# Grouping four dense tiles of the delta rule's preparation into two visits of two

## The reference

```python
def chunk_gated_delta_rule(q, k, v, g, beta):
    ...
    decay = jnp.exp(jnp.where(causal, g[..., :, None] - g[..., None, :], -jnp.inf))
    lower = jnp.where(strict, jnp.einsum('bhncd,bhnmd->bhncm', k_beta, k) * decay, 0.0)
    a_mat = lower + jnp.eye(C, dtype=jnp.float32)
    rhs = jnp.concatenate([v_beta, k_beta * jnp.exp(g)[..., None]], axis=-1)
    sol = lax.linalg.triangular_solve(a_mat, rhs, left_side=True, lower=True, unit_diagonal=True)
    ...
    qk = jnp.einsum('bhncd,bhnmd->bhncm', q, k) * decay
    ...
# in the same layer, independent of the delta rule:
gate_b, gate_c, hv = sc_in[..., :SC_WIDTH], sc_in[..., SC_WIDTH:2 * SC_WIDTH], sc_in[..., 2 * SC_WIDTH:]
y = gate_b * causal_depthwise_conv(gate_c * hv, sc_conv_w)
```

## Time and profile before

| | us |
|---|---|
| median of 3 runs | 3553.3 (3548.85, 3553.3, 3554.7) |
| the profiled execution, its own time | 3546.45 |
| its span, first to last instruction | 3544.6 |
| preparation of the first layer, on PE | 2293.3 to 2328.0 |
| preparation of the second layer, on PE | 2972.2 to 3006.9 |

### The profile page before, as it was taken

One profiled execution on the slowest core, in us unless ns is written; L12 is line 12 of the kernel. 1 busy time (PEld: TensorE's weight loads), 2 busy tenths in 40 slices (PEclk: granted clock), 3 DMA queues, 4 the chain that ended last, 5 costly groups with the idle time before them and its releaser, 6 DMA issues. The chain is left out here.

```text
span 3544.6 us, 44743 instructions
## 1 busy us (share of the span) xinstructions
PE 3472.5 (98%) x18492; PEld 2827.2 (80%) x18492; DVE 1985.0 (56%) x2961; ACT 1203.7 (34%) x1890; POOL 149.8 (4%) x212
## 2 busy tenths in 40 slices
PE   9999999999999999999999999999999999999999
PEld 6878877688888888877688887788888888788887
DVE  5565576775466755666763366675423366652233
ACT  3222334632233222334632234633322254342222
POOL 1110100001000110100000001000000000000000
PEclk9999999999999999999999999999999999999999
DMA  8663341245343653331333242212233322123332
GB/s 287 220 196 115 96 106 48 90 152 188 124 153 114 215 177 115 98 104 49 90 121 124 87 154 57 72 37 78 84 96 119 101 61 66 43 73 100 95 98 87
DMA packets 438048, 397.84 MB, mean 112 GB/s; under 512 B 53780, under 2 KB 390276, under 8 KB 437845
## 3 DMA queue, kind: packets, MB, share of 16 engines
q1 hardware_dynamic: 413028, 310.53, 29.0%
q0 software_dynamic: 24816, 84.45, 7.0%
HBM read 390.14 MB, written 4.78 MB: 111 GB/s over the span
## 5 line engine op out<-in xcount | busy, mean ns | idle before, releaser
L175 PE MATMUL m_ps<-m_h_high,ffn_w_high 128*128 128x512 f32 x2064 | 806.8, 391 | 4.9 <-DVE ffn_w_low L182 4.9
L177 PE MATMUL m_ps<-m_h_high,ffn_w_low 128*128 128x512 f32 x2064 | 803.6, 389 | 0.0
L176 PE MATMUL m_ps<-m_h_low,ffn_w_high 128*128 128x512 f32 x2064 | 803.3, 389 | 0.0
L175 PEld LDWEIGHTS m_ps<-m_h_high,ffn_w_high 128*128 128x128 f32 x2064 | 387.4, 188 | 87.4 <-issue 7.1
L177 PEld LDWEIGHTS m_ps<-m_h_high,ffn_w_low 128*128 128x128 f32 x2064 | 387.4, 188 | 81.2
L176 PEld LDWEIGHTS m_ps<-m_h_low,ffn_w_high 128*128 128x128 f32 x2064 | 387.6, 188 | 79.2
L1062 ACT ACTIVATE ffn_sil<-m_ps 128x512 f32<-128x512 f32 x132 | 79.0, 599 | 1087.4 <-PE m_ps L177 1087.4
L175 PE MATMUL m_ps<-ffn_w_high,ffn_hid_high 128*128 128x512 f32 x1056 | 411.6, 390 | 0.0
L177 PE MATMUL m_ps<-ffn_w_high,ffn_hid_low 128*128 128x512 f32 x1056 | 411.0, 389 | 0.0
L176 PE MATMUL m_ps<-ffn_w_low,ffn_hid_high 128*128 128x512 f32 x1056 | 410.9, 389 | 0.0
L182 DVE TENSOR_TENSOR ffn_w_low<-m_raw,ffn_w_high 128x2048 fp32r<-128x2048 f32 (+1 forms) x138 | 296.3, 2150 | 120.2 <-ACT ffn_w_high L1056 117.4
(11 more groups left out here) (511 smaller groups left out, 5375.4 us busy)
## 6 DMA issues: line engine op xcount, KB each, us to landing
m_raw<-in_ffn_w SPq DMA_DIRECT2D x176, 512.0 KB, 4.8
ffn_rows<-in_ada_w POOLq DMA_DIRECT2D x128, 512.0 KB, 5.0
ffn_rows<-in_ffn_w SPq DMA_DIRECT2D x88, 512.0 KB, 3.5
m_raw<-in_w_in SPq DMA_DIRECT2D x32, 1024.0 KB, 5.2
m_raw<-in_ffn_w_gate SPq DMA_DIRECT2D x44, 512.0 KB, 3.7
m_raw<-in_ffn_w_up SPq DMA_DIRECT2D x44, 512.0 KB, 4.8
ffn_rows<-in_ffn_w_down SPq DMA_DIRECT2D x44, 512.0 KB, 3.3
m_raw<-in_w_out SPq DMA_DIRECT2D x24, 512.0 KB, 4.4
```

Source lines behind the costliest of these rows:

```text
L175: pe.matmul(out, sh, mh, start=first, stop=False, skip_group_check=True)
L176: pe.matmul(out, sh, ml, start=False, stop=False, skip_group_check=True)
L177: return pe.matmul(out, sl, mh, start=False, stop=last, skip_group_check=True)
```

## The change

On PE the call of `dense` behind every token tile goes; behind token tiles 1 and 3 (the second and the fourth) two dense tiles are now computed, 0 and 1, then 2 and 3. On ACT `evacuate` stands in turns 1 and 3, for both tiles. On DVE it stands in turn 2 for tiles 0 and 1, and behind the loop for tiles 2 and 3. No instruction is added or taken away, and no buffer changes.

```diff
@@ PE, end of the turn of token tile i
                 mm.then_inc(S.v_turned, 1)
-                dense(i)
+                if i % 2:
+                    dense(i - 1, i)
@@ ACT, turn i
                 act.activation(A.D[:, i], A.D[:, i], ACT.Exp).then_inc(S.decay, 1)
-                evacuate(i)
+                if i % 2:
+                    evacuate(i - 1)
+                    evacuate(i)
                 act.wait_ge(S.q_scaled, i + 1)
@@ DVE, turn i, between diff and the lower triangle
-                if i:
+                if i and i % 2 == 0:
+                    evacuate(i - 2)
                     evacuate(i - 1)
                 dve.wait_ge(S.decay, i + 1)
@@ DVE, behind the four turns
+            evacuate(TT - 2)
             evacuate(TT - 1)
```

## The result

Over nine runs of each, the changed kernel takes 3563.3 us in the median and the kernel before 3550.9: +12.4 us, ratio 1.0031 with a 95% interval of 1.0022 to 1.0039. It is slower, by 0.2 to 0.4%. The forecast was 12.4 us more than before.

A forecast was written before the change was run, and what follows sets the result against it. PE, busy 98% of the span, was taken as the bound. Per layer 6.57 us of waits - 0.54 for the mask + 0.19 small terms gave 6.2, for two 12.4: 3565.7 us against median 3553.3, range 3558 to 3573.

The forecast's parts named there:

- PE sets the end, DVE's chain is covered by the dense tiles: Four turns: only PE's idle time counts; dense tiles (5.55 us) hide DVE's 6.5 us chain, token tiles take PE 3.45.
- Token tile 1, 2.68 us: Second token tile, uncovered: PE waits for DVE's differences, lt_ready, nat_ready and prep_free, 2.68 us a layer in all.
- the 10.4 that I named: Expected profile row: PE's waits at L2748 on DVE's second triangle product, 5.2 us a layer (1.7 and 3.6).
- Token tile 3, 3.89 us, and the 2.86 us of DVE work in it: Fourth token tile: PE waits 3.89 us a layer; low part, copy and low part put 2.86 us before tile 2's triangle.
- The short waits for `nat_ready` and `prep_free`: Before each dense pair, PE waits 0.18 us for one DVE product and 0.15 us for the next.
- The mask, -0.54: Start of the levels: PE's old wait on DVE's first mask (L2784) goes, -0.54 us a layer.
- Small terms, +0.19: Slower first instructions behind seven new waits, less a missing changeover in each dense pair: together +0.19 us a layer.
- the 0.35 us for restarts: First instruction behind a wait takes 0.65 instead of 0.60 us; seven new waits give +0.35 us.
- The sum: Both layers together: 6.2 us a layer, 12.4 us in all, giving 3565.7 us against the earlier median.
- Rival A: Levels and behind: PE's existing waits take up the delay, leaving 3.1 us in all, 3556.4 us; chance 0.10.
- the counter-argument: Against regained waits: L175's 1.5 us and the recurrence's waits depend on PE's own earlier work, so they move with it.
- Rival B: Token tile 3: PE's clock halves behind the 3.56 us wait, +3.0 us a layer, 18.4 in all, 3571.7 us; chance 0.06.

The follow-up runs named there:

- e2_evac_only: Kernel before, with only the ACT and DVE evacuations moved as in the change, dense tiles left behind every token tile; 3558.6 us, ratio 1.0029 to before.
- e4_filled: Changed kernel, with unread constant products filling PE's waits for lt_ready in token tiles 1 and 3; 3558.6 us, ratio 1.0024 to the kernel before.
- e3_low_behind: Changed kernel, with DVE's evacuations of tiles 0 and 1 moved behind token tile 2's last product; 3558.8 us, ratio 1.0031 to the kernel before.
- e6_cast_behind: Changed kernel, with ACT's evacuation of tile 1 behind the exponential of token tile 2's rows, tile 3's behind the turns; one run, 3562.55 us.
- e1_pe_only: Kernel before, with only PE's dense tiles grouped in two visits of two, evacuations left; 3579.1 us, ratio 1.0082 to before.

## Why the prediction was right

- *PE sets the end, DVE's chain is covered by the dense tiles*: right. e2_evac_only, which leaves the dense tiles in place, has no wait in any token tile; each kernel that moves them has waits in tiles 1 and 3, or in e4_filled the products put in their place.
- *Token tile 1, 2.68 us*: right. The pair starts 8.38 us behind the first turned rows where 8.31 were forecast (second layer). The waits in the brackets are shorter than mine (0.44 instead of 0.67, 1.46 instead of 1.68) because the two are counted differently. The bracket counts from start plus length of the instruction before; I counted from where the next would have started, which is some 0.2 us earlier (four transposes have a length of 0.60 us and take 0.36 or 0.44 to the next start). By the starts the waits are 0.68 (2298.26 to 2299.30, less 0.36) and 1.67 us (2299.30 to 2301.41, less 0.44). That is also why L2748 has 8.7 us in the list and not the 10.4 that I named.
- *Token tile 3, 3.89 us, and the 2.86 us of DVE work in it*: right. The bracket has 3.36 us, by the starts it is 3.52 (3006.31 to 3010.27 in the second layer, less 0.44), and 3.56 were forecast. The short waits for `nat_ready` and `prep_free`, 0.18 and 0.15 forecast, have no row in the list of waits, but from start to start L2758 and L2763 take 0.12 and 0.16 us more in token tile 3 than in token tile 2. That the second pair ends 21.89 us behind the first, to the hundredth as forecast, is in part luck, since small terms cancel in it. e3_low_behind took 2.1 us out of this wait and gave 0.77 back; e6_cast_behind took 0.5, since the rows' own sums are ready only that much sooner than the cast ends.
- *The mask, -0.54*: too small. The levels became shorter by 0.74 to 0.79 us in the profiles of the changed kernel. I had taken 0.54 from the bracket, and all the new waits from the starts. By the starts the old one is larger too: the eight instructions of L2784 that hold it take 1.55 us to the next dense tile (2334.36 to 2335.91), without it 0.79 (2346.63 to 2347.42).
- *Small terms, +0.19*: wrong in size. The preparation without a costly fall is 41.26 us; 34.72 + 6.57 is 41.29, so the small terms together are -0.03. Of the 0.35 us for restarts only some 0.1 shows: from L2748 to the pair it is 3.41 and 3.40 us in token tiles 1 and 3, and 3.35 by my times. Token tile 2 takes 0.08 more (3.53 instead of 3.45), and each pair 0.1 less (10.99 and 11.00 instead of 11.1). Together the clean layer is 5.76 us instead of 6.22.
- *The sum*: 12.4 forecast, 12.4 measured. The waits without the clock give 11.5; the clock can give the rest, though no run resolves its size. That the total meets the forecast to the tenth is partly luck: the mask and the small terms were 0.46 us a layer too dear together, and the clock, put at nothing, made up for them.
- *Rival A*, the delay taken up later: fell. 0.78 of 5.21 us were regained, and PE is still idle for 2.72 us in the levels. The waits at L175 (3.0 us in all) and the recurrence (26.6 us) stayed as they were, so they moved with PE, as the counter-argument said.
- *Rival B*, the clock: it did happen, in part, and 0.06 was too little for it. I had priced it as 3.0 us for every layer, in token tile 3; it was 2.6 in the first layer of both profiles, in token tiles 1 and 3, and next to nothing in the second. One of the signs that I had named for a wrong forecast, matmuls of twice their length behind the wait in token tile 3, is there in the first layer (L2758 in 1.92 us), and my granted clock of 1.00 was 0.92 and 0.96. So the time was forecast better than the mechanism: the waits are the larger part, and a second cost that I had put at nothing goes with them. My ground for thinking it unlikely, that the clock had not fallen behind the 2.36 us in the one profile I had, didn't hold: in other executions it falls just there (e4_filled).
- *Where the two piece moves stand*: the forecast took both as one. e1_pe_only shows that the evacuations' move takes away a good part of the cost of the dense tiles' move: from about 31 to 12.4 us in time, from 10.4 to 5.8 us a layer without the clock. Alone (e2_evac_only) it costs 5 us of waits and some 6 us more, as much as the falls of the clock in its profile can give.

## What to carry to other kernels

Work of the bounding engine that depends on nothing nearby is cover for another engine's chain; before grouping it, compare the chain's length with what is left between its pieces (here 6.5 us against 3.45), and write the difference down as a wait in each uncovered place. What an engine has queued between two links of the chain, such as splits and casts for later, belongs under the cover that is left, not between the links, as far as its inputs are there by then. And look for a wait of the bounding engine that comes from mere order on another: two independent steps behind four short ones, instead of ahead of them, gave 2.5 us a layer and a kernel faster than both.

## What the runs showed of the hardware

- PE's clock fell to half behind idle stretches much shorter than I had expected: behind 2.36 us (e4_filled, second layer: L2735 in 1.02 instead of 0.65 us), and behind 1.99 us (e2_evac_only: a dense tile at a mean clock of 0.76, 1.6 us longer). It is not the same each time. The 2.36 us were followed by slow matmuls in the second layer of seven of eight profiles and in the first layer of one. No rule for this comes out of the runs.
- What a fall costs depends on what stands behind it: 1.6 us before full work (e2_evac_only), next to nothing if PE would have waited anyway (changed kernel, second layer). So a stretch of waits hides falls that the same wait ahead of covered work would show.
- On one core the scatter of a kernel's runs, 3541.9 to 3558.0 us here, goes for the most part with the granted clock: 3.1 us for 0.001 of its mean, and a standard deviation of 1.7 us around the line instead of 3.5.
